# Turning the sample keys on VectorE in 32x32 blocks in a one-core hybrid decoder layer

## What is computed

```python
x = x + 0.5 * swiglu_ffn(x, ffn1...)                    # 1024 -> 2*2816 -> 1024
h = rmsnorm(x); u, q, k, v, qm = split(h @ w_in)          # 2048 columns
y_pool = pool_mixer(u)                                    # windows 2, 4, 8, 16
q, k = rotary(rmsnorm(q)), rotary(rmsnorm(k))             # 8 heads x 64
# block-sparse attention: own block and the top 3 past blocks of 256 keys by q . mean(key)
y_moba = softmax(q @ keys of the chosen blocks) @ values
y_mem = softmax(qm @ mk) @ mv                             # 4 heads, 256 memory tokens
x = x + concat(y_pool, y_moba, y_mem) @ w_out
x = x + 0.5 * swiglu_ffn(x, ffn2...)
```

## Time and profile before

| | us |
|---|---|
| median of 3 runs | 660.12 (658.65 to 660.78) |
| the profiled execution | 658.21, of which 656.4 are its span |
| PE busy | 629.0 (96%) |
| DVE busy | 377.7 (58%) |
| ACT busy | 281.6 (43%) |
| POOL busy | 12.0 (2%) |
| DMA | 128.25 MB, mean 195 GB/s |

### The profile page before, as it was taken

How to read it: one execution, slowest core, us unless ns; L and a number is a source line. 1 busy time by engine, 2 the same in 40 slices (tenths; PEclk the granted TensorE clock), 3 DMA queues, 4 the chain that set the end, 5 groups by cost and what they waited for, 6 DMA issues and landing times.

```text
span 656.4 us, 13652 instructions
## 1 busy us (share of the span) xinstructions
PE 629.0 (96%) x5168; PEld 569.2 (87%) x5168; DVE 377.7 (58%) x666; ACT 281.6 (43%) x446; POOL 12.0 (2%) x21
## 2 busy tenths in 40 slices
PE   5999999999999999899899999899999999999997
PEld 3999998998999978467567776799999999989997
DVE  4476677767644555538344264236877667774443
ACT  5734343344533455145263363336533443343331
POOL 1000000000000010000000000002100000000000
PEclk9999999999999999899899999999999999999999
DMA  9967786766686431577677993306656565646521
GB/s 275 269 198 242 226 241 185 237 198 215 220 268 205 172 114 52 180 230 267 237 230 234 306 363 129 139 22 172 193 164 188 163 186 165 191 163 224 189 96 67
DMA packets 132705, 128.25 MB, mean 195 GB/s; under 512 B 6648, under 2 KB 103815, under 8 KB 132655
## 3 DMA queue, kind: packets, MB, share of 16 engines
q1 hardware_dynamic: 132375, 127.60, 61.7%
q10 hardware_dynamic: 288, 0.08, 0.1%
HBM read 124.95 MB, written 2.83 MB: 195 GB/s over the span
## 4 chain that ended last, share of the span: by engine, by line
PE 82%; DVE 9%; ACT 4%; issue 2%; DMA 1%; DVEq 0%; SPq 0%; ACTq 0%
PE banks L1210 23%; PE banks L1211 21%; PE banks L1212 21%; PE banks L1218 7%; DVE w_lo L853 3%; PE banks L1331 2%; PE banks L1589 2%; ACT w_hi L577 2%; PE banks L1514 2%; PE banks L1533 1%; DVE x_lo L866 1%; DMA raw<-in_ffn_w_in 1%; DVE xT L874 1%; DMA x_rows<-in_x_prompt 1%; DVE kv L859 1%
## 5 line engine op out<-in xcount | busy, mean ns | idle before, releaser
L853 DVE TENSOR_TENSOR w_lo<-raw,w_hi 128x1024 fp32r<-128x1024 f32 x160 | 195.8, 1232 | 154.8 <-ACT w_hi L577 154.5
L1210 PE MATMUL banks<-x_hi,w_hi 128*128 128x264 f32 x768 | 223.3, 291 | 5.0 <-DVE w_lo L853 3.8
L1211 PE MATMUL banks<-x_lo,w_hi 128*128 128x264 f32 x768 | 219.0, 285 | 0.0
L1212 PE MATMUL banks<-x_hi,w_lo 128*128 128x264 f32 x768 | 218.9, 285 | 0.0
L577 ACT ACTIVATE w_hi<-raw 128x1024 fp32r<-128x1024 f32 x160 | 162.9, 1050 | 78.4 <-PE banks L1212 71.5
L1210 PEld LDWEIGHTS banks<-x_hi,w_hi 128*128 128x128 f32 x768 | 145.9, 190 | 10.2 <-DVE w_lo L853 5.1
L1211 PEld LDWEIGHTS banks<-x_lo,w_hi 128*128 128x128 f32 x768 | 146.2, 190 | 0.0
L1212 PEld LDWEIGHTS banks<-x_hi,w_lo 128*128 128x128 f32 x768 | 145.5, 190 | 0.0
L1210 PE MATMUL banks<-h_hi,w_hi 128*128 (+1 forms) x352 | 100.2, 285 | 1.5 <-DVE h_tmp L889 1.5
L1212 PE MATMUL banks<-h_hi,w_lo 128*128 (+1 forms) x352 | 100.1, 284 | 0.0
L1211 PE MATMUL banks<-h_lo,w_hi 128*128 (+1 forms) x352 | 100.0, 284 | 0.0
(11 more groups left out here) (236 smaller groups left out, 545.0 us busy)
## 6 DMA issues: line engine op xcount, KB each, us to landing
raw<-in_ffn_w_in SPq DMA_DIRECT2D x88, 512.0 KB, 4.5
raw<-in_ffn_w_out SPq DMA_DIRECT2D x44, 512.0 KB, 3.5
kv<-in_cache_k SPq DMA_DIRECT2D x64, 256.0 KB, 4.3
kv<-in_cache_v SPq DMA_DIRECT2D x64, 256.0 KB, 4.4
raw<-in_w_in SPq DMA_DIRECT2D x12, 512.0 KB, 3.3
raw<-in_w_out SPq DMA_DIRECT2D x8, 512.0 KB, 4.6
raw<-in_mem_w_kv SPq DMA_DIRECT2D x4, 512.0 KB, 3.3
raw<-in_w_in SPq DMA_DIRECT2D x8, 256.0 KB, 2.8
```

The costliest lines, as they stand in the source:

```text
L853: vec.tensor_tensor(w_lo[:, n % RING, :], raw[:, n % RING, :], w_hi[:, n % RING, :].bitcast(F32), ALU.subtract).then_inc(lo_ready, 1)
L1210: pe.matmul(out, lhs[0], rhs[0], start=start, stop=False)
L1211: pe.matmul(out, lhs[0], rhs[1], start=False, stop=False)
L1212: return pe.matmul(out, lhs[1], rhs[0], start=False, stop=stop)
```

## The change

- The 64 key pages are no longer turned by TensorE. VectorE transposes each pair of pages in place (128 x 1024 floats, in blocks of 32x32): 12 pairs beside the output part of the first FFN, 4 in rounds 1 and 2, 16 in rounds 7 to 11. Banks 0 and 1 become free for the prompt heads (`LANES`).
- A partition then holds one channel of 32, of 4 groups of 32 tokens. The queries become block-diagonal: 4 groups x 8 columns. `K` b has 16 matmuls with 256 columns, for 32 channels each, and sequences 0 to 3 and 4 to 7 go to the two halves of one bank. The queries are turned once more by a small matmul with a repeated identity, and VectorE fills `q_cols` in two times of 16 copies.
- A sequence's logits of a head lie in four rows. Sums and maxima are joined over these by a matmul with the mask `same`, the sums of the exponentials by a second. Masks are built by VectorE in round 2.
- Value pages are loaded so that a page goes to 32 partitions, four pieces of 2 KB in each, where it went to 128 partitions. `V` has as many matmuls as before, with 8 columns in place of 32.
- The low part of units 4 to 19 of this stage (`W`) is made by GpSimd.
- Prompt heads run earlier: `HA` 5 and 6, `HB` 4 and 5, `PV` 4 and 5 lie in rounds 14 and 15 and no longer in the tail.

```diff
-K_BANKS, LG_BANK, MISC = (0, 1), 2, 6
-LANES = (6, 6, 6, 6, 6, 4, 5, 6, 4, 5, 6, 1)
+LG_BANK, V_BANKS, MISC = 2, (3, 2), 6
+LANES = (0, 1, 0, 1, 0, 1, 0, 1, 0, 1, 5, 6)
+EARLY_PAIRS = 12
         EXTRA = {
...
+            4: {3: [("NQ", 2)], 4: [("QT", 0)], 6: [("QT", 2), ("NV", 2)]},
+            5: {1: [("ND", 2)], 2: [("NS", 2)], 3: [("K", 0)], 4: [("NG", 2)], 6: [("K", 1)]},
+            6: {2: [("T", 0)], 3: [("K", 2)], 5: [("T", 1)], 6: [("K", 3)]},
+            7: {1: [("QF", 1)], 2: [("E", 3), ("NQ", 3), ("G", 16)], 3: [("G", 17)], 4: [("E", 4), ("NV", 3)], 5: [("ND", 3), ("G", 18)],
+                6: [("E", 5), ("NS", 3), ("G", 19)]},
+            8: {1: [("NG", 3), ("NQ", 4)], 2: [("K", 4)], 3: [("NV", 4)], 4: [("ND", 4), ("OWN", 0)], 5: [("NS", 4)], 6: [("G", 20)]},
+            9: {1: [("NG", 4)], 2: [("OWN", 1)], 3: [("G", 21)], 4: [("G", 22), ("T", 2)], 5: [("G", 23), ("T", 3)], 6: [("G", 24)]},
+            10: {1: [("K", 5), ("G", 25)], 2: [("HA", 0), ("HA", 1)], 3: [("HM", 0), ("G", 26)], 4: [("HM", 1), ("HE", 0), ("G", 27)], 5: [("HE", 1)],
+                 6: [("K", 6), ("G", 28)]},
+            11: {1: [("HB", 0), ("G", 29)], 2: [("E", 6), ("HT", 0), ("HB", 1)], 3: [("HT", 1), ("G", 30)], 4: [("E", 7)], 5: [("G", 31)], 6: [("E", 8)]},
+            12: {1: [("K", 7), ("PV", (0,))], 2: [("HV", (0,)), ("PV", (1,))], 3: [("HV", (1,)), ("A", 0), ("HA", 2)], 4: [("HA", 3)],
+                 5: [("A", 1), ("HM", 2)], 6: [("A", 2), ("HE", 2)]},
+            13: {1: [("HM", 3), ("A", 3)], 2: [("HE", 3)], 3: [("A", 4), ("HB", 2)], 4: [("HT", 2)], 5: [("A", 5), ("HB", 3), ("PV", (2,))],
+                 6: [("HT", 3), ("HV", (2,))]},
+            14: {1: [("V", 0), ...
...
+                    at_ = t % 4 * 32
+                    sp.dma_start(kv[at_:at_ + 32, slot, t // 4 * 2048:(t // 4 + 1) * 2048].rearrange("k (b c) -> k b c", b=4),
+                                 cache[0, ds(page, 1)].rearrange("o (b k) h d -> k (o b) (h d)", b=4)).then_inc(kv_loaded[slot], 16)
...
+            pool.wait_ge(lo_ready, U_WIN + 4)
+            for what, k in steps():
+                if what == "W":
+                    n = U_WIN + k
+                    pool.wait_ge(hi_ready, n + 1)
+                    pool.tensor_tensor(w_lo[:, n % RING, :], raw[:, n % RING, :], w_hi[:, n % RING, :].bitcast(F32),
+                                       ALU.subtract).then_inc(lo_ready, 1)
...
+            def turn_pair(g):
+                kv_wait(vec, "k", g // 4)
+                vec.transpose(key_pair(g), key_pair(g)).then_inc(k_turned8, 1)
...
-            ffn_out_loop(0, 1, 5)
+            for n in range(16):
+                split(U_OUT[0] + 2 + 4 + n)
+                if n < EARLY_PAIRS:
+                    turn_pair(n)
...
+            def query_fill(half):
+                for b in range(4):
+                    for c in range(4):
+                        off = 32 * c + 8 * b + c // 2 * 4
+                        some = vec.tensor_copy(q_cols[32 * b:32 * b + 32, :].rearrange("p (b x) -> p b x", b=4)[:, :, off:off + 3 * P + 1:P],
+                                               q_all[32 * b:32 * b + 32, 4 * c:4 * c + 4, 4 * half:4 * half + 4].rearrange("p h b -> p b h"))
+                some.then_inc(q_filled, 1)
...
+                pe.wait_ge(k_turned8, 4 * (b + 1))
+                half, b4 = b // 4, b % 4
+                keys = kv[:, b % KV_SLOTS, :].rearrange("p (t c k) -> p c t k", t=PAGES, c=16)
+                for c in range(4):
+                    for hp in range(4):
+                        c0 = 512 * b4 + P * hp + 32 * c
+                        mm = pe.matmul(bank[LG_BANK][32 * hp:32 * hp + 32, half * NP:(half + 1) * NP], q_cols[:, c0:c0 + 32],
+                                       keys[:, 4 * hp + c], start=(b4 == 0 and c == 0), stop=(b4 == 3 and c == 3))
```

More of the change, by code:

```diff
@@ L64 @@
 J_ORDER = (2, 3, 0, 1)
[L65 removed]
+M_EARLY = (4, 5, 6, 7, 0, 1, 3)
 SQ_AFTER = (1, 3, 5)
@@ L100, in shape_constants @@
     c["delta"] = delta
-    back = np.zeros((P, NS), np.float32)
+    back = np.zeros((P, 2, NS), np.float32)
     for r in range(P):
-        if r % 32 < 2 * NS:
-            back[r, r % 32 // 2] = 1.0
+        for half in range(2):
+            back[r, half, 4 * half + r % 4] = 1.0
     c["back"] = back
@@ L1079, in _ @@
             for what, k in steps():
-                if what == "W":
-                    split(U_WIN + k)
-                elif what == "G" and k not in ACT_PAGES:
+                if what == "G":
+                    turn_pair(k)
+                elif what == "MG" and k not in ACT_PAGES:
                     key_evac(k)
+                elif what == "QF":
+                    vec.wait_ge(k_used, 4)
+                    query_fill(1)
                 elif what == "SS":
@@ L1325, in key_logits @@
                     pe.wait_ge(res_ready, KT)
-                for side in range(2):
-                    pe.wait_ge(kT_ready[side], PAGES // 2 * (b + 1))
-                keys = kv[:, b % KV_SLOTS, :].rearrange("p (t c k) -> p c t k", t=PAGES, c=4)
-                for half in range(2):
-                    for c in range(4):
-                        mm = pe.matmul(bank[LG_BANK + half][32 * c:32 * c + 32, :], q_cols[:, c, b, :],
-                                       keys[:, c, 4 * half:4 * half + 4, :], start=(b == 0), stop=(b == NS - 1))
+                elif b == 4:
+                    pe.wait_ge(q_filled, 2)
@@ L1464, in _ @@
                     mm.then_inc(qm_turned, 1)
+                elif what == "QT" and k == 2:
+                    pe.wait_ge(q_apart, 1)
+                    pe.matmul(bank[MISC][:, P:2 * P], repeat[:], q_spread[:].rearrange("p c n -> p (c n)"), start=True, stop=True)\
+                        .then_inc(q_turned, 1)
                 elif what == "QT":
@@ L1473, in _ @@
                     pe.wait_ge(own_ready, 1)
-                    pe.matmul(bank[MISC][:, 0:1], own_e[:].rearrange("p h m -> p (h m)"), ones[0:NS, 0:1], start=True, stop=True)\
-                        .then_inc(own_psum, 1)
+                    for half in range(2):
+                        mm = pe.matmul(bank[MISC][:, half:half + 1], own_e[:, half].rearrange("b h p t c -> b (h p t c)"), ones[0:NS, 0:1],
+                                       start=True, stop=True)
+                    mm.then_inc(own_psum, 1)
                 elif what == "POOL" and k == 0:
```

318 lines of the change are left out of this document (181 added, 137 removed), and 25 rows, old and new, of tables (EXTRA, TAIL).

## The result

The changed kernel takes **652.75 us** (median of 9 runs, 644.24 to 656.36). Beside it on the same chip the kernel before took 658.65 (median of 9). The ratio is **0.9857**, interval [0.9825, 0.9888]: 9.4 us less than 660.12 (7.4 to 11.6), where the prediction had 22.1. By the medians beside each other it is 5.9 us, by the two profiled spans 5.4 (656.4 and 651.0). It is faster, as forecast, and inside the range of 624 to 657; but the gain is less than half of the forecast, and the likeliest case's own range, 630 to 646, doesn't hold it. (Ratios here are formed from the runs within 1.5% of each kernel's fastest, medians from all runs; where the two differ a little, this is why.) The profiled execution has a span of 651.0.

The account below looks back on a forecast made before the run. TensorE's queue was taken to set the time. 36.6 us saved, less 1.0 added work, 6.0 VectorE's order, 2.5 softmax, 3 GpSimd, 2 clock, gave 22.1 less: 638 us against the median of 660.1, range 624 to 657.

Parts of the forecast that it names:

- the likeliest case: Whole kernel: the forecast of 638 us, own range 630 to 646, chance 0.50.
- What goes from TensorE's path: Key-page transposes 28.2 us, waits for page copies 5.0, slow clock behind these 3.4: 36.6 us less.
- what comes: TensorE's added work: shorter K matmuls, repeat, `same` matmuls, own product, less four transposes: net 1.0 us.
- The transpose: VectorE's turn of one 128x1024 pair: taken as 1.23 us, like a low part; bounds half of that to 6.9.
- rival 4: VectorE's transposes cost 2.5 us or more each, so the kernel is not faster: 661 or 676 us; chance 0.15.
- VectorE's order: Rounds 7 to 11: TensorE stops 2.5 us before K 4, 3 before T 2, 0.5 for the rest; 6.0 together.
- the softmax's join: Softmax of the samples: two matmuls now stand in the chain, so TensorE waits 2.5 us at A 4.
- The lock: GpSimd's splits in rounds 3 to 14 hold up VectorE's two-tile operations: 3 us on the path, 0 to 8.
- Rival 2: GpSimd and VectorE hold each other up; TensorE's stops grow to 4 or 5 us: 649 us; chance 0.15.
- Clock: Slow TensorE clock behind stops of 2.5 to 3 us, some 1.7 each but not every time: 2 us.
- rival 3: Value pages from V 4 on load half as fast to 32 partitions, costing 0 to 10 us: 643; chance 0.10.
- What would show it: Signs for the forecast: transposes 1.1 to 1.3 us, rounds about 122 to 126, tail about 46, GpSimd splits 2.2 to 3.

Follow-up runs that it names:

- dve_spread: Changed kernel with low parts of units 4 to 19 on VectorE and each value page loaded to every fourth partition: 634.04 us, ratio 0.9618.
- low_on_dve: Changed kernel with the low parts of units 4 to 19 back on VectorE, all else as changed: 638.75 us, ratio 0.9703.
- warm: Changed kernel with TensorE's idle time at five waits filled by matmuls without use, every wait kept: 645.40 us, ratio 0.9822.
- values_wide: Changed kernel with value pages loaded to all 128 partitions as before: 646.63 us, ratio 0.9800.
- pairs_short: Changed kernel with low parts on VectorE and pairs 16 to 31 turned in 32 of 1024 columns only: 640.24 us, ratio 0.9634.
- all_together: Changed kernel with low parts on VectorE, value pages on every fourth partition, earlier turns, ScalarE query-fill copies and TensorE fillers: 633.21 us, ratio 0.9593.
- early_turns: Changed kernel with low parts on VectorE, TensorE fillers, pairs 16 and 17 turned in round 6, second query-fill copies on ScalarE: 640.07 us, ratio 0.9695.

## Why the prediction was right and wrong, step by step

- **What goes from TensorE's path (36.6 us), and what comes (1.0).** Right as far as it can be told. A sequence of K takes 1.86 us for 1.85. In dve_spread, where neither the hold nor slow transfers disturb, 36.6 - 1.0 less its stops at K 4, T 2 and the join (3.0 + 2.8 + 1.7) is 28.1; measured by its ratio 25.2. The 2.9 between have room in the clock: it is 0.94 there over 120.2 us of rounds, a shortfall from full clock of at most 7.2 us, part of it while TensorE stood idle. That the sum comes out within 3 us doesn't show each term.
- **The transpose.** Taken at 1.23 us out of 0.6 to 6.9, measured at 1.225: the nearest row, a low part of the same size, was the right guide, and rival 4 is out. The Trainium skill's figure gave 1.07 as an estimate ("Vector Engine (DVE) Microarchitecture Reference", section 3.8); the measurement is 0.15 above it. Twelve pairs beside the first FFN cost at most 0.5 us: the waits for low parts are 4.3 for 3.8 us over the whole program.
- **VectorE's order (6.0 us of stops) and the softmax's join (2.5).** Right in place. In size the sum fits once the hold is away, and that is partly luck: low_on_dve stops for 3.0 before K 4 (forecast 2.5), 4.4 before T 2 (3) and 1.4 at the join (2.5), 8.8 for 8.5 with the 0.5 for the rest, and it has the low parts on VectorE, which the forecast had not. In the changed kernel they are 4.1, 2.9 and 3.4, and with K 0 and `QT` 14.7.
- **The lock (3 us, 0 to 8): this is the step that failed.** Put back, the low parts give 14 us by the medians and 10 by the ratios, where the sum had 3 and at most 8. I scaled: 1.1 us lost in 4.15 of GpSimd's, hence 8 us, of which 3 on the path. The count was too low by half (17.6 us held); beside the kernel before, where VectorE has fewer short operations, the same splits hold it for 8.3, so the count was about right for the kernel that the rows came from. The earlier trace rows show three short operations of GpSimd between four long ones of VectorE, each holding the other in turn, and most of the loss on GpSimd's side. Here the long operation is GpSimd's, and it falls on VectorE's short ones: a copy of 0.23 us costs 2.3. A ratio taken from one pairing of lengths says nothing of another. The share on the path was too low as well: I counted the norms of rounds 4, 5 and 7 to 10, and neither the mask and the fills ahead of `QT` and K 0 nor the softmax. VectorE is partly idle there, but the chain to TensorE's next step runs through its small operations, whether it is busy or not. Rival 2 (649) named the mechanism, and of the times written down its is the nearest; its stops of 4 to 5 us in four rounds are not what came (4.1 before K 4, the others 2 to 3.4), so the closeness is in part luck.
- **Clock (2 us).** Too low: 7 by the medians of warm, 5.5 in the stretch of its profiled run, though 2.3 by its ratio. The mechanism was in the earlier trace rows (some 1.7 us behind a stop) and was applied to one stop or so out of what became five. It isn't wholly a cause beside the hold: in low_on_dve, with stops of 8.8 for 14.7 us, the profiled clock is 0.988 for 0.976.
- **The value pages (rival 3, 0.10).** The mechanism is true: 8.7 us to land for 4.4, 220 to 240 GB/s with the DMA engines full for 374. In the changed kernel all that is to be seen is a gap of 0.9 us at V 5, which the profile puts down to nothing, though by values_wide the whole price was about 4 to 6. With the low parts back on VectorE it is 4.7 us (638.75 to 634.04). That it hides the gains in the rounds is shown in part only: pairs_short has 5.0 us of waits for transfers where its gain should be, but all_together, with the same early turns and value pages that land in time, is just 0.8 us below dve_spread.
- **GpSimd's time, 2.2 to 2.9 us a unit.** Right, 2.38.
- **What would show it.** Rounds at 122 to 126 us: 131.8 in the changed kernel, 119.8 in low_on_dve. Tail at about 46: 48.3, and 44.6 in dve_spread.
- **What the sum left at nothing: the rest of the program.** The profiled runs, cut at the first matmul of the projection and at the first of the output mixing:

| | us before | between | behind |
|---|---|---|---|
| before | 228.2 | 198.4 | 229.8 |
| after | 228.7 | 187.9 | 234.4 |
| warm | 228.2 | 182.4 | 232.5 |
| values_wide | 227.3 | 184.2 | 232.7 |
| low_on_dve | 227.6 | 176.8 | 231.2 |
| early_turns | 228.2 | 174.3 | 233.8 |
| dve_spread | 227.7 | 173.6 | 230.7 |
| all_together | 228.2 | 171.9 | 230.3 |

Between the two the change gains 10.5 us in these runs; behind them, in the same output mixing and second FFN, the changed kernel loses 4.6. Its clock there is 0.96 over the first 40 us, where the kernel before has 1.00. Why it is lost stays open; one profile of each kernel can't say whether it belongs to the kernel or to the execution. Differences of 2 or 3 us between two whole times are thus not safe to lay on an edit.

Added up for the changed kernel between these two points: 35.6 - 14.7 (stops, of them 0.6 for the queries counted already) - 5.5 (clock, by warm) - 0.9 (V 5) = 14.5 or 15.1, measured 10.5. Some 4 to 5 us stay without an owner; slower loads that push work later without a wait of their own are a candidate (values_wide gains 3.6 there), which isn't proved. The sizes of hold and clock overlap too: of the 11.0 us that low_on_dve gains there, 5.9 are stops, and the rest isn't parted further.

## What to carry to other kernels

Work given to GpSimd is free only while VectorE's short copies and two-input operations near it are on no chain that TensorE waits for; price it, as an upper bound, by GpSimd's whole duration for each short operation that it can meet, not by a share of busy time measured in another program. When a change makes one engine the pace-setter in a stretch, each new stop can cost TensorE more in slow clock behind it, and not the same in every execution. Compare a stop only together with what ran ahead of it. Where the placement of data is changed, look at which partitions one transfer reaches: every fourth did as well as all, 32 neighbours did not, and the price stayed hidden until the other waits were gone.

## What the runs showed of the hardware that I had not expected

- An operation of VectorE of 0.23 us (128x128 copy) took 2.29 beside a GpSimd subtraction and 0.94 beside a GpSimd copy; a VectorE transpose of 128x1024 took 1225 ns in the changed kernel and 1227 in low_on_dve (means of 32), and one that ran wholly beside a GpSimd subtraction (at 287.75 us, within 287.61 to 289.97) took 1.25 us, so it isn't held.
- GpSimd copies 128x1024 floats in 1.05 us and subtracts them in 2.38.
- 256 KB to 32 neighbouring partitions landed in 8.7 to 12.4 us (medians of a run, the longest in pairs_short), to every fourth in 4.2, to neighbours in alternating halves in 6.8.
- After a stop of 3.0 us the same 32 matmul records took 1.93 us in low_on_dve and 3.19 in dve_spread.
- Executions of one program differed by 12 us (644.24 to 656.36) with their mean clock (0.992 to 0.971); with the gaps filled five of six lay within 1.5 us, and the sixth, at clock 0.981, 8 us above them.
